# Gate and up projections of two FFNs as 2x2 block products by Strassen's method (seven products per weight slab in place of eight)

## What is computed

```python
FFN_DIM = 4 * D_MODEL                              # D_MODEL = 1024

def macaron_ffn(x, g_pre, w_gate, w_up, w_down, g_post):
    n = rms_norm(x, g_pre)
    f = (jax.nn.silu(n @ w_gate) * (n @ w_up)) @ w_down
    return x + 0.5 * rms_norm(f, g_post)
```

## Time and profile before

| | |
|---|---|
| median of three runs | 1780.87 us |
| the profiled execution | 1788.5 us, its span 1786.4 us |
| TensorE (PE) matmuls | 12258, busy 1694.8 us (95%) |
| VectorE (DVE) busy | 836.7 us (47%) |
| ScalarE (ACT) busy | 501.2 us (28%) |
| GpSimd (POOL) busy | 57.7 us (3%) |
| mean granted TensorE clock | 0.971 of full speed |
| DMA | 158.60 MB, mean 89 GB/s |

### The profile page before, as it was taken

How to read it: one execution, slowest core, us unless ns; L and a number is a source line. 1 busy time by engine, 2 the same in 40 slices (tenths; PEclk the granted TensorE clock), 3 DMA queues, 4 the chain that set the end, 5 groups by cost and what they waited for, 6 DMA issues and landing times.

```text
span 1786.4 us, 28331 instructions
## 1 busy us (share of the span) xinstructions
PE 1694.8 (95%) x12258; PEld 1643.8 (92%) x12258; DVE 836.7 (47%) x1086; ACT 501.2 (28%) x695; POOL 57.7 (3%) x69
## 2 busy tenths in 40 slices
PE   7999999999999979997989989799999999999996
PEld 6999999999999979996879749699999999999995
DVE  4443443344334457999555432744334333433345
ACT  4222232232122243121543323432122222212221
POOL 3000000000000000004010010000000000000000
PEclk8999999999999989998999989899999999999997
DMA  4322222222222231323233532032222222223221
GB/s 138 119 72 95 72 94 71 75 92 90 76 72 94 71 102 48 104 69 120 95 125 116 187 144 68 27 95 71 95 72 94 71 94 70 94 70 94 70 70 53
DMA packets 137865, 158.60 MB, mean 89 GB/s; under 512 B 3197, under 2 KB 130769, under 8 KB 137768
## 3 DMA queue, kind: packets, MB, share of 16 engines
q1 hardware_dynamic: 131648, 136.06, 23.8%
q0 software_dynamic: 6032, 21.19, 3.3%
q10 hardware_dynamic: 96, 0.02, 0.0%
HBM read 152.22 MB, written 5.40 MB: 88 GB/s over the span
## 4 chain that ended last, share of the span: by engine, by line
PE 84%; DVE 12%; ACT 2%; issue 1%; DMA 1%; POOL 0%; DVEq 0%; ACTq 0%; POOLq 0%
PE slot L1249 78%; DVE f L1072 6%; DVE R L909 1%; PE slot L1296 1%; PE slot L1288 1%; DVE f L929 1%; DVE wp L894 1%; PE slot L1481 1%; DVE h L933 1%; PE slot L1500 1%; DVE n L915 0%; DMA kring<-in_cache_mem_v_dram 0%; ACT wp L554 0%; DMA graw<-in_conv_ln_b_dram 0%; PE slot L1272 0%
## 5 line engine op out<-in xcount | busy, mean ns | idle before, releaser
L1249 PE MATMUL slot<-n,wp 128*128 128x288 f32 x7296 | 995.0, 298 | 42.0 <-DVE n L915 31.4
L1249 PEld LDWEIGHTS slot<-n,wp 128*128 128x128 f32 x7296 | 983.0, 190 | 50.6 <-issue 39.2
L554 ACT ACTIVATE wp<-raw 128x1024 fp32r<-128x1024 f32 x232 | 246.2, 1061 | 1054.0 <-PE slot L1249 1039.3
L1249 PE MATMUL slot<-mid,wp 128*128 128x288 f32 x3840 | 515.2, 296 | 4.6 <-issue 2.9
L1249 PEld LDWEIGHTS slot<-mid,wp 128*128 128x128 f32 x3840 | 514.0, 190 | 5.2 <-issue 5.2
L894 DVE TENSOR_TENSOR wp<-raw,wp 128x1024 fp32r<-128x1024 f32 x232 | 284.1, 1225 | 158.3 <-ACT wp L554 158.3
L984 DVE TENSOR_TENSOR f<-slot,f 128x576 f32<-128x576 f32 x64 | 48.4, 757 | 245.9 <-PE slot L1249 245.9
L945 DVE TENSOR_TENSOR sil<-slot,R 128x576 f32<-128x576 f32 x68 | 51.2, 757 | 236.2 <-PE slot L1249 236.1
L971 DVE TENSOR_TENSOR sil<-slot,sil 128x576 f32<-128x576 f32 x64 | 48.5, 758 | 191.2 <-PE slot L1249 191.2
L1072 DVE SCALAR_TENSOR_TENSOR f<-glu,convw,f 128x512 f32<-128x512 f32 x240 | 111.7, 542 | 0.0
L1272 PE MATMUL slot<-memT,raw 128*128 128x256 f32 x256 | 56.0, 379 | 0.0
(11 more groups left out here) (192 smaller groups left out, 564.4 us busy)
## 6 DMA issues: line engine op xcount, KB each, us to landing
raw<-in_ffn_w_gate_dram SPq DMA_DIRECT2D x32, 1024.0 KB, 5.5
raw<-in_ffn_w_up_dram SPq DMA_DIRECT2D x32, 1024.0 KB, 5.5
raw<-in_ffn_w_down_dram SPq DMA_DIRECT2D x32, 1024.0 KB, 5.0
raw<-in_mix_w_in_dram SPq DMA_DIRECT2D x8, 1024.0 KB, 5.6
kring<-in_cache_mem_k_dram POOLq DMA_DIRECT2D x6, 1024.0 KB, 5.7
kring<-in_cache_mem_v_dram POOLq DMA_DIRECT2D x6, 1024.0 KB, 5.5
raw<-in_xattn_w_k_dram SPq DMA_DIRECT2D x4, 1024.0 KB, 5.0
raw<-in_xattn_w_v_dram SPq DMA_DIRECT2D x4, 1024.0 KB, 5.0
```

The source lines that it names most:

```text
L554: nc.scalar.activation(wp[:, J % 2, 0], raw[:, s % RAW, :, (J % 2) * P:(J % 2 + 1) * P], ACT.Copy)\
L1249: ins = pe.matmul(slot(u)[:, half, 0:HALF], wp[:, J % 2, wi, kt], X(xi, kt, half), start=kt == 0 and k == 0, stop=kt == KT - 1 and k == le ...
```

## The change

In an FFN, 4 of block 0's 8 gate and up slabs stay jobs as before (two pairs). Each of the other 28 slabs becomes a group, computed by the Winograd form of Strassen's method. A slab's weights (1024 x 256) are cut into 2 x 2 blocks: contraction halves of 4 tiles, column halves of 128 (A11, A12, A21, A22). The tokens are cut into contraction halves and token halves of 288 (B11 to B22). A plain job pair makes 8 block products of 4 x 3 matmuls each; a group makes 7 (P1 to P7), from sums of blocks:

- the weights of P5 and P7 (`q13`: A22 + A21 and A11 + A21), of P6 (`q2`) and of P3 (`q4`) are sums that VectorE makes for every slab; P1, P2 and P4 take blocks as they are. All seven are split into high and low parts, into `wu`.
- the token operands of the seven products (`nb`) are made once per FFN, in `first_pair` and `second_pair`: tokens times gain times `R` into `f` (normalised, so nothing is scaled afterwards), the four blocks split, then turned into sums and split again.
- P1 runs in one bank; ScalarE copies it out, P6 is added on top, copied, P7, copied, P4. P5 and P3 share a second bank and P2 has a third. VectorE adds copies and banks: C11 = P1 + P2, C22 and C12, C21 with their signs.
- the first down job of a block is laced into the last group. The beginning of the next block (`start_groups`) makes its first weights when the last down jobs are done, since `wu` lies over `wp`.
- `f` isn't zeroed any more (block 0's down outputs are copied); the memory's load moves to FFN 1's end, since `nb` takes the place of the tile it shared.

The operands' places, and the slab loads on SP:

```diff
+P1, P5, P6, P2, P7, P4, P3 = range(7)
...
-        wp = sb("wp", [P, 2, PARTS, KT, P], PDT)
...
+        rw = views("region_w", [("wp", [P, 2, PARTS, KT, P], PDT), ("kT", [P, KT, MEM], F32), ("vtok", [P, MT, D], F32)],
+                   [("wu", [P, 7, PARTS, KH, P], PDT), ("q13", [P, 2, KH, P], F32)],
+                   [("wp_", [P, 2, PARTS, KT, P], PDT), ("b12", [P, PARTS, KH, HALF], PDT)])
...
+            def load_after_group(s, src, name, g, b):
+
+                sp.wait_ge(q4_lo, group_count(name, g, b))
                 sp.dma_start(raw[:, s % RAW], src).then_inc(loaded[s % RAW], 16)
```

ScalarE's order over the groups of a block (a `high_` makes a high part, a `copy_` brings a product out of PSUM):

```diff
+                def groups(g0, b):
+                    for g in range(g0, GROUPS):
+                        last, after_up = g == GROUPS - 1, g % 2 == 0 and g > g0
+                        if last:
+                            prepare(J0 + 16, b, (p5_done, group_count(name, g, b)))
+                        copy_p6(g, b)
+                        if g % 2:
+                            silu_rest(g - 1, b)
+                        elif after_up:
+                            high_first(g - 1, b)
+                        if last:
+                            prepare(J0 + 17, b, (p2_done, group_count(name, g, b)))
+                        else:
+                            high_q2(g + 1, b)
+                        copy_p7(g, b)
+                        if not last:
+                            act.wait_ge(p7_done, group_count(name, g, b))
+                            high_q13(g + 1, b)
+                            wait_c11(g, b)
+                            copy_p1(g + 1, b)
+                        if after_up:
+                            high_second(g - 1, b)
+                        if not last:
+                            act.wait_ge(p4_done, group_count(name, g, b))
+                            high_a2(g + 1, b)
+                        if g % 2 == 0:
+                            silu_c21(g, b)
+                        if g + 2 < GROUPS:
+                            act.wait_ge(p1_done, group_count(name, g + 1, b))
+                            high_a11(g + 2, b)
+                        if not last:
+                            act.wait_ge(job_done, J0 + 2 * g + 2 + b * JOBS_PER_BLOCK)
+                            high_q4(g + 1, b)
```

VectorE at the beginning of an FFN, and at the beginning of a block's groups (`seventh` and `eighth` are what is left of the last two jobs; in ScalarE's `start_groups`, `high_q13` and `high_q2` wait for the last job's end, and `copy_p1` stands behind `high_q2`):

```diff
+                def first_pair():
...
+                    for t in range(KT):
+                        V.scalar_tensor_tensor(out=f[:, t], in0=h[:, t], scalar=gain[g_pre][t], in1=R[:, :],
+                                               op0=ALU.mult, op1=ALU.mult).then_inc(normed, 1)
+                    take_scaled(sil[:, 0], J0, u0)
+                    take_scaled(sil[:, 1], J0 + 1, u0 + 1)
+                    prepare(J0 + 3)
+                    for e in range(2):
+                        scale_gate(name, e)
+                    dve.wait_ge(normed, KT * (STAGE[name] + 1))
+                    b_low(0, nb[:, P1], B11)
+                    b_low(1, b12, B12)
+                    b_low(2, nb[:, P2], B21)
+                    b_low(3, nb[:, P3], B22)
+                    for e in range(2):
+                        dve.wait_ge(gate_scaled, GATE0[name] + e + 1)
+                        multiply(2 + e, e)
+                        prepare(J0 + 4 + e)
...
+                def start_groups(g, b, seventh, eighth):
+
+                    sum_q13(g, b)
+                    seventh()
+                    low_a11(g, b)
+                    low_q13(g, b)
+                    sum_q2(g, b)
+                    low_q2(g, b)
+                    eighth()
+                    low_a2(g, b)
+                    sum_q4(g, b)
+                    low_a11(g + 1, b)
+                    low_q4(g, b)
```

TensorE: a product, the waits of the seven, and a block's order:

```diff
+                def product(p, dst, start, marks):
...
+                    for kt in range(KH):
+                        for k, (wi, xi) in enumerate(PRODUCTS):
+                            ins = pe.matmul(dst[:, 0:HALF], wu[:, p, wi, kt], nb[:, p, xi, kt],
...
+                def p1(g, b, first):
+                    wait_slot(pe, group_use(name, g), 6 * b)
...
+                    pe.wait_ge(a11_lo, group_count(name, g, b))
+                    product(P1, x_bank(g), True, [p1_done])
+
+                def p5(g, b):
+                    pe.wait_ge(q13_lo, group_count(name, g, b))
...
+                def p6(g, b):
+                    pe.wait_ge(p1_copied, group_count(name, g, b))
+                    pe.wait_ge(q2_lo, group_count(name, g, b))
...
+                def p2(g, b):
+                    wait_slot(pe, group_use(name, g) + 1, 6 * b)
+                    pe.wait_ge(a2_lo, group_count(name, g, b))
...
+                def p7(g, b):
+                    pe.wait_ge(p6_copied, group_count(name, g, b))
...
+                def p4(g, b):
+                    pe.wait_ge(p7_copied, group_count(name, g, b))
...
+                def p3(g, b):
+                    pe.wait_ge(c22_done, group_count(name, g, b))
+                    pe.wait_ge(q4_lo, group_count(name, g, b))
...
+                    p1(g0, b, True)
+                    p5(g0, b)
+                    for g in range(g0, GROUPS - 1):
+                        p6(g, b)
+                        p2(g, b)
+                        p7(g, b)
+                        p1(g + 1, b, g == g0)
+                        p4(g, b)
+                        p3(g, b)
+                        p5(g + 1, b)
...
+                    first = start_job(name, 16, b)
+                    down_part(*first, range(0, 4))
+                    p4(g, b)
+                    down_part(*first, range(4, 6))
+                    p3(g, b)
+                    second = start_job(name, 17, b)
+                    down_part(*second, range(0, 6))
+                    down_part(*first, range(6, 8))
+                    down_part(*second, range(6, 8))
```

More of the change, by code:

```diff
@@ new lines, in build, with normed_to @@
+        sums["cmean"] = {"summed": sem("cmean_summed")}
+        sums["cvar"] = {x: sem(f"cvar_{x}") for x in ("squared", "recip", "summed")}
+        PER_NORM = {"squared": KT, "recip": 1, "summed": 3, "hi": KT, "ready": KT, "scaled": KT, "done": KT}
+        def normed_to(s, x, count):
+            if s[0] != "p":
+                return sums[s][x], count
+            each = (4 if s.startswith("pre") else KT - 2) if x == "added" else PER_NORM[x]
+            return sums[s][x], (int(s[-1]) - 1) * each + count
@@ L1001, in ffn @@
-                down(BLOCKS - 1, True)
+                last = BLOCKS - 1
+                groups(0, last)
+                for i in range(KT):
+                    take_down(i, last)
+                    prepare(J0 + 16 + i + 2, last)
+                    add_square(post, i)
+                    if beside and i == 5:
+                        beside()
             for i in (1, 3):
@@ L1347, in ffn @@
+                jobs_normed(name, pre, 4, mid)
+                pe.wait_ge(b_lo, 8 * STAGE[name] + 4)
+                for i in range(4, 8):
+                    job(name, i, operand)
+                pe.wait_ge(b_lo, 8 * STAGE[name] + 8)
+                block_of(4, 0)
                 with pe.Fori(1, BLOCKS) as b:
-                    with pe.Fori(0, 2) as j:
-                        for i in range(8):
-                            job(name, i, half_of(n), b=b, j=j)
-                    down(b)
+                    block_of(0, b)
```

640 lines of the change are left out of this document (469 added, 171 removed).

## The result

The changed kernel took **1734.63 us** (median of 4 runs, 1730.75 to 1736.76) where the kernel before took 1784.86 in the same comparison: a ratio of 0.9716, 95% interval 0.9669 to 0.9764. The profiled execution took 1736.76 us (span 1735.0), 51.7 less than the one of before. The prediction was 1735.7, in a range of 1710 to 1766, and faster by over 1% with a chance of 0.85.

The account below looks back on a forecast made before the run. TensorE, busy 95%, was taken as the bound: 89.6 us saved less 24.4, 10.6, 7.4 and 2 lost leaves 45.2, so the profiled 1788.5 becomes 1743.3, or 1735.7 from the median 1780.87; range 1710 to 1766.

Parts of the forecast that it names:

- 672 matmuls at 0.1333: Both FFNs: 56 groups issue 12 matmuls fewer each, at 0.1333 us a matmul, 89.6 us less.
- Beginning, jobs 3 and 4: Start of each FFN: TensorE waits for VectorE's normalising, low parts and weights before jobs 3 and 4; 7.8 us lost each.
- Beginning, group 4: First group of each FFN: waits of 0.9 at P5, 2.8 at P6, 0.6 at P2; 4.4 us lost.
- Between blocks: Behind the last down job: waits at P5, P6, P2 and P7, 1.8 us six times, 10.6 us lost.
- Job 18: Down jobs: its weights take 2.5 us from job 16's end, job 17 covers 1.6; 0.9 x 8 blocks, 7.4 us.
- Clock: Lower clock behind the pause before group 4's P6: 1.5 us lost, counted as 1 an FFN, 2 in all.
- the rival that would have eaten the gain: Steady state: VectorE becomes the bound, a pair takes 24.0 us for 22.4, 45 us, giving 1780; the 1752 to 1785 case had 0.19.
- the clock in steady state: Rival: waits between products keep TensorE's clock low, a group takes 20.2 us, 9.0 more; chance 0.06.
- the bank term: Products write one bank twelve in a row; nearest rows differ by 0.8%, 5 us either way on 4704 matmuls; taken as 0.
- The chains cost half: Rival: ScalarE and VectorE start early, halving the 42.4 us of waits; 21 us less, 1715; chance 0.13.
- Slower than before: Outcome of the low-clock rival: with a quarter of the 56 groups slow, 1862 us; chance 0.05.
- doesn't do what it says: Rival that the matmuls are not saved; ruled out beforehand, as the built program has 4272 an FFN for 4608.

Follow-up runs that it names:

- experiment 8: Changed kernel with four more VectorE additions of 512 elements in each of FFN 2's 28 groups: 1763.03 us.
- experiment 1: Changed kernel with VectorE doing the two scalings and job 3's weights ahead of the eight normalising instructions at each FFN's start: 1743.16 us.
- experiment 4: Changed kernel with VectorE's three instructions for `mid` moved to where it idles or among group 5's weights, ScalarE's high part moving along: 1728.06 us.
- experiment 6: Changed kernel with ScalarE waiting for the last down job ahead of `high_q13` at every block's end, not in block 0 alone: 1737.09 us.
- experiment 7: Changed kernel with TensorE's loop over blocks 1 to 3 written out, so no jump between blocks; other engines keep their loops: 1729.07 us.
- experiment 5: Changed kernel with the second down job cut after tile 4 instead of 5, leaving three tiles behind the first job's last two: 1728.66 us.

## Why the prediction was right

By the two profiled executions the gain was 51.7 us, against a sum of 45.2; by the medians of the comparison it was 50.2. The predicted time came out within 1.1 us all the same, because it was taken from 1780.87, the median of three runs, and that kernel's median was 1784.86 with a fourth run and between 1777.74 and 1787.22 in later comparisons. The prediction put most of the 7.6 us between its profile and that median down to FFN 1's idle time; no other execution of the kernel before was profiled, so no run shows that. The agreement of the totals is partly luck, then, and the terms tell more. In us:

| Term | Predicted | In the profile after |
|---|---|---|
| 672 matmuls at 0.1333 | -89.6 | -89.6; 0.1330 each in a stretch |
| Beginning, jobs 3 and 4 | +15.6 | +15.3 (job 4 at 17.9 instead of 10.2, twice) |
| Beginning, group 4 | +8.8 | +7.4 (0.98 at P5, 2.7 at P6, none at P2) |
| Between blocks | +10.6 | 0 for the waits; +7.0 for four pauses |
| Pauses and lower clock of before in FFN 1 | not counted | -3.2 (its stretch less FFN 2's, rows 2) |
| Job 18 | +7.4 | +8.3 |
| Clock | +2 | +4.8 (three stretches of 1.6) |
| Sum | -45.2 | -50.0; the profiles differ by 51.7 |

A pause counts here by the step from one matmul to the next, less 0.133; its row's idle time is some 0.16 less. In FFN 1 of the kernel before, 4.9 us of idle time and 1.5 of lower clock made its stretch only 3.2 us longer than FFN 2's, since the block between its two pauses ran at 0.130 a matmul (756 from 341.90 to 440.18 us); why, no run shows. The waits between blocks and the pauses in their place have nothing in common but the place, so that 7.0 came for 10.6 is luck too.

- **What goes, and the steady state.** Right. A matmul that is not issued is worth its 0.133 us, since nothing else becomes the bound: VectorE is busy 80% where 80 to 90 was said, and experiment 8 puts its need at 19.15 of 22.4 us a pair, between the 18.0 of the sum and the 24.0 of the rival that would have eaten the gain. That rival, the clock in steady state and the bank term are all answered by one row, 955 matmuls in 127.00 us at granted clock 1.00.
- **The beginning.** Right to 0.1 us in its chain. What looks like a loss of 6.3 us at job 3 is the place where VectorE's chain happens to be waited for (experiment 1). The place of group 4's wait was right too, but its reason only half: the prediction named ScalarE's order, and with that mended the wait moved to P7 and then to P4. It went when VectorE's three instructions for `mid` went from there (experiment 4).
- **Between blocks: the step that failed.** "P5 waits as above (0.9), P6 for `q2` until 4.5 instead of 4.1 (0.4), P2 for `low_a2` ... 1.8 x 6 = 10.6 us." None of it is there. ScalarE's wait for the last down job ahead of `high_q13` stands under `if third:`, which only block 0's beginning passes; elsewhere `q13` is split a job earlier. (The section on the change says without that condition that `high_q13` waits for the last job's end; it holds for block 0 alone.) With the wait put there P5's and P6's sizes are right (0.82 and 0.29, experiment 6). It was a misread order, not a wrong duration. In its place came TensorE's own jumps, 7.0 us, which the prediction did not price. The kernel before has a loop as well, and its idle time in FFN 1, which stands at the loop's two turns (experiment 7), was carried along as it stood; that it too comes from the jump was not tried.
- **Job 18.** Right, 0.9 predicted and 0.98 to 1.13 measured, and its reason shown by experiment 5.
- **The clock.** Mechanism right, size too small: of the 1.5 us lost behind P6, 1 was counted in each FFN, with a credit for VectorE's lag, and the slower matmuls cost 1.6. The stretch behind one of the pauses was not foreseen. At 477.9 it lies inside blocks 1 to 3, where the prediction named a clock of 0.50 as a sign of being wrong; it was one stretch of 3.4 us, not the steady state.
- *The chains cost half* would have been 1715: the chains at the beginning cost what was said. *Slower than before* and *doesn't do what it says* did not come.

## What to carry to other kernels

When a matmul-bound stage loses matmuls, price the saving by the stage's own spacing, and then look for the loss at the seams: at the beginning, at the block's turn and where buffers change hands, not in the steady state. A wait that an edit removes is gone only if the engine behind it has room; if the wait moves on at full size, as from P6 to P7 to P4 here, take work off that engine instead of reordering the one that waits for it. Read the order of each seam under its own conditions (first block, loop, last block), and look in the trace at what each jump back of an engine costs: it was nothing at two turns here and 1.5 to 1.9 us at four.
